# Sigmoids of the mixing stage made from tanh, gate columns moved forward in the input projection, forget-gate logarithm placed behind the decay chain

## The chip, the core and the metric

The kernel runs on one core of a Trainium2 chip. TensorE multiplies matrices into eight PSUM banks, VectorE (DVE) and ScalarE (ACT) do elementwise work, GpSimd (POOL) does elementwise work in SBUF and issues some DMAs, SyncE (SP) issues the weight loads. Each engine runs its own list of instructions; semaphores order them. The metric is the device time of one launch in microseconds.

## The reference

Two layers of a hybrid encoder over 288 tokens, 256 of a prompt and 32 of a second request. In each layer, with width 1024:

```python
x = x + 0.5 * swiglu(rmsnorm(x, n1), f1g, f1u, f1d)
z = rmsnorm(x, nm) @ w_in_l
logf = jax.nn.log_sigmoid((ff + b_f).astype(F32))
o_fox = (o_fox.reshape(B, T, FOX_WIDTH) * jax.nn.sigmoid(fg)).astype(x.dtype)
...
w = -jax.nn.softplus(-(w0 + jnp.tanh(wd) @ w_up).astype(F32)) - 0.5
decay = jnp.exp(-jnp.exp(w))
a = jax.nn.sigmoid((a0 + ad @ a_up).astype(F32))
g = (jax.nn.sigmoid(gd) @ g_up).astype(F32)
kk = kk * lax.rsqrt(jnp.maximum(jnp.sum(kk * kk, axis=-1, keepdims=True), 1e-24))
k = k * (1.0 + (a - 1.0) * k_a.astype(F32).reshape(RWKV_HEADS, HEAD_DIM))
bonus = jnp.sum(r * k * r_k.astype(F32)[None, None], axis=-1, keepdims=True) * v
...
o = head_norm(o, RET_GN_EPS).reshape(B, T, RET_WIDTH) * jax.nn.silu(g.astype(F32))
...
x = x + jnp.concatenate([o_fox, o_rwkv.astype(x.dtype), o_ret.astype(x.dtype)], axis=-1) @ w_out_l
x = x + 0.5 * swiglu(rmsnorm(x, n2), f2g, f2u, f2d)
```

The three mixers are a forgetting attention of 8 heads (fox), an RWKV-7 time mixing of 4 heads, and a chunkwise retention of 4 heads. A last gate and a norm end the layer.

## The kernel before

Everything is float32 and stands feature by feature in the partitions, with the 288 tokens along the free dimension. A weight matrix comes in slots of 1 MB through a ring of four buffers. Each product is made of three: a slot is cast to a high part (ScalarE) and a remainder (VectorE, in the projection GpSimd), and so is the activation, and TensorE adds high by high, high by low and low by high.

The input projection has 31 blocks of 128 columns (`NZ`). For block n, `z_cast(n)` on ScalarE (L563) makes the high part of the weights, `rest(n)` on GpSimd (L419) the remainder, TensorE does 24 matmuls (`z_slot`, L1320 and L1323) into one of four banks, and `z_copy(n)` on ScalarE (L575) brings the bank into the tile `zT`. There are two pairs of weight buffers, so the cast of block n waits until TensorE is through block n-2, and GpSimd waits for the cast. On ScalarE the first 16 blocks are a loop of two turns (L577). The last four blocks, 27 to 30, are the output gate of the attention (`Z_FG`); ScalarE takes Exp of their negative instead of a copy (L574).

Work of the RWKV mixer is put by hand between the blocks:

- VectorE shifts blocks 0 to 6 in time (L871 to L879). ScalarE then takes Exp of the small block (L593, `esm`), VectorE makes a sigmoid of it (`sigmoid_of`, L851 and L852) and scales it (L885, `lowin`). TensorE's low-rank products for decay and learning rate wait for it behind block 17 (L1337).
- VectorE prepares the keys (L890) and the forget gate (L894 to L896). ScalarE squares the keys (L596), then takes Exp and Ln for the forget gate (L599, L600), and casts block 19.
- ScalarE takes Exp of the four low-rank outputs (L605, `e_low`, tile `sig4`). TensorE goes on with blocks 18 and 19, makes the gate's low-rank products and the head sums of the squared keys (L1348), and goes on with blocks 20 to 23.
- VectorE: the forget-gate chain (L898 to L910: logarithm, three cumulative sums, a copy, two products into `foxL`), which the attention wants much later; then the sigmoids of `sig4` (L851, L852), the logarithm of the decay and its cumulative sums (L917 to L924), the clamp of the key norm (L930, which signals `kln`), and, once ScalarE has the inverse norm (L617, L618), the keys (L932 to L936) and the input of the bonus (L939, which signals `bonin`).
- TensorE, behind block 23: two rotation products for the retention (L1355), which wait for `kln` since they take the clamped banks, then two bonus products (L1364), which wait for `bonin`; then blocks 24 to 29, two more rotations and block 30. ScalarE takes the four decay exponentials (L622 to L627) between its blocks 22 and 23.

After that come transposes, the products inside a chunk, four levels of a triangular inverse (TensorE L1429 to L1441, VectorE L1016 to L1027, where `sigmoid_of` is also applied to the four blocks of `Z_FG`, one in each level), the recurrence over nine chunks, the attention and the output projection. VectorE's `link` makes an instruction wait for the end of the one before it.

## Time and profile before

| | |
|---|---|
| median of three runs | 1635.5 us (1634.3 to 1638.49) |
| profiled execution, its own time | 1637.02 us |
| its span from first to last instruction | 1635.4 us |
| TensorE busy | 1539.1 us, 94% of the span |
| VectorE busy | 867.2 us, 53% |
| ScalarE busy | 593.8 us, 36% |
| GpSimd busy | 196.8 us, 12% |
| mean granted clock of TensorE | 0.920 |

A row of the trace in order of time has the start and the duration in microseconds, the engine, the line of the kernel, the operation, output and inputs with their shapes, how many instructions are merged in the row, and in brackets how long the engine was idle before and what ended that. Instructions of one line that follow each other stand in one row, with the time from the first's start to the last's end. A busy TensorE is not TensorE at its peak: its matmuls are pipelined and their ends are modelled. The granted clock is 1.0 at 2.4 GHz and 0.5 at 1.2 GHz.

### The profile page before, as it was taken

To read this page: it belongs to the slowest core of one execution; us is meant where nothing else is said; L and a number is where in the kernel's file an instruction comes from. 1 tells how busy PE (TensorE), PEld (TensorE's weight loads), DVE (VectorE), ACT (ScalarE), POOL (GpSimd) and SP (SyncE) were. 2 spreads that over 40 slices of the span, in tenths; PEclk is the share of its full clock that TensorE was granted. 3 is DMA by queue.
4 is the path that set the end of the run, shared out by engine and by line. 5 is a ranking of instruction groups with operands and counts; after the bars stand their busy time and mean duration, and the time that the engine had idled before them with its cause. 6 is when DMAs were issued, how large, how long until landed. Compare 5 with 4: busy or idle time off the path is not lost. (4 is left out here: it accounts for less than half of the span.)

```text
span 1635.4 us, 27385 instructions
## 1 busy us (share of the span) xinstructions
PE 1539.1 (94%) x11276; PEld 1428.3 (87%) x11276; DVE 867.2 (53%) x1240; ACT 593.8 (36%) x871; POOL 196.8 (12%) x129
## 2 busy tenths in 40 slices
PE   7999999988989999999979999997899999999997
PEld 6999989877755899999979999897787568999997
DVE  4555344768444445553555553348773543555535
ACT  4334334441023444433443342445220334443324
POOL 1000017640020000000000000275400200000000
PEclk9999999988667999999989999999985779999999
DMA  7444433430010244444334444243300122444443
GB/s 300 157 162 172 154 129 129 155 114 20 11 59 27 101 156 173 161 158 177 133 134 154 166 168 156 102 157 126 133 1 11 59 75 107 145 164 156 178 158 133
DMA packets 32035, 209.81 MB, mean 128 GB/s; under 512 B 4392, under 2 KB 6072, under 8 KB 7752
## 3 DMA queue, kind: packets, MB, share of 16 engines
q1 hardware_dynamic: 29392, 200.39, 34.1%
q0 software_dynamic: 2560, 8.26, 1.4%
q8 instruction: 58, 0.95, 0.3%
q14 instruction: 25, 0.20, 0.0%
HBM read 204.54 MB, written 4.10 MB: 128 GB/s over the span
## 5 line engine op out<-in xcount | busy, mean ns | idle before, releaser
L792 DVE TENSOR_TENSOR split_w<-wc,split_w 128x2048 fp32r<-128x2048 f32 x140 | 320.6, 2292 | 374.4 <-ACT split_w L519 374.4
L519 ACT ACTIVATE split_w<-wc 128x2048 fp32r<-128x2048 f32 x140 | 268.4, 1917 | 540.5 <-PE bank L1252 341.7
L1246 PE MATMUL bank<-split_x,split_w 128*128 128x288 f32 x2816 | 399.1, 299 | 15.8 <-ACT split_x L525 15.8
L1246 PEld LDWEIGHTS bank<-split_x,split_w 128*128 128x128 f32 x2816 | 385.7, 190 | 21.0 <-ACT split_w L519 13.7
L1269 PE MATMUL bank<-split_x,split_w 128*128 (+1 forms) x2112 | 282.2, 295 | 0.0
L1269 PEld LDWEIGHTS bank<-split_x,split_w 128*128 128x128 f32 x2112 | 281.8, 188 | 0.0
L1252 PE MATMUL bank<-split_x,split_w 128*128 128x288 f32 x1408 | 202.2, 296 | 0.0
L1252 PEld LDWEIGHTS bank<-split_x,split_w 128*128 128x128 f32 x1408 | 192.6, 189 | 0.3 <-DVE split_w L792 0.3
L419 POOL TENSOR_TENSOR split_x<-wc,split_x 128x1024 fp32r<-128x1024 f32 x32 | 79.8, 2493 | 509.0 <-ACT split_x L563 509.0
L563 ACT ACTIVATE split_x<-wc 128x1024 fp32r<-128x1024 f32 x62 | 65.4, 1059 | 111.6 <-PE bank L1323 111.6
L1320 PE MATMUL bank<-split_h,split_x 128*128 128x288 f32 x496 | 84.4, 313 | 7.5 <-ACT split_h L568 7.4
L1320 PEld LDWEIGHTS bank<-split_h,split_x 128*128 128x128 f32 x496 | 74.0, 196 | 12.3 <-issue 9.0
L1320 PE MATMUL bank<-split_x 128*128 128x288 f32 x496 | 79.8, 305 | 0.0
L419 POOL TENSOR_TENSOR split_e<-wc,split_x 128x1024 fp32r<-128x1024 f32 x30 | 75.5, 2517 | 25.2 <-ACT split_x L563 25.2
L1320 PEld LDWEIGHTS bank<-split_x 128*128 128x128 f32 x496 | 72.8, 195 | 0.7
L818 DVE SCALAR_TENSOR_TENSOR et<-et,bank 128x288 f32<-128x288 f32 x88 | 40.0, 454 | 45.8 <-PE bank L1252 45.8
L1728 PE MATMUL bank<-split_x,split_w 128*128 128x288 f32 x384 | 53.0, 298 | 0.0
L1728 PEld LDWEIGHTS bank<-split_x,split_w 128*128 128x128 f32 x384 | 51.7, 189 | 1.1 <-ACT split_x L757 1.1
L411 POOL DMA_DIRECT2D extra<-srwkv_in x2 | 1.3, 658 | 359.0 <-issue 348.2
L1323 PE MATMUL bank<-split_h,split_x 128*128 128x288 f32 x256 | 40.4, 301 | 0.0
L1323 PEld LDWEIGHTS bank<-split_h,split_x 128*128 128x128 f32 x256 | 37.1, 195 | 0.0
L1323 PE MATMUL bank<-split_h,split_e 128*128 128x288 f32 x240 | 36.8, 296 | 0.0
(291 smaller groups left out, 1681.5 us busy)
## 6 DMA issues: line engine op xcount, KB each, us to landing
wc<-wcol SPq DMA_DIRECT2D x174, 1024.0 KB, 4.8
wc<-wfirst SPq DMA_DIRECT2D x12, 1024.0 KB, 4.9
con<-consts_in SPq DMA_DIRECT2D x1, 2230.0 KB
arena<-kc_in POOLq DMA_DIRECT2D x8, 256.0 KB, 3.1
arena<-vc_in POOLq DMA_DIRECT2D x2, 1024.0 KB, 5.1
xT<-x_in SPq DMA_DIRECT2D x2, 576.0 KB, 4.4
k_out<-zT POOLq DMA_DIRECT2D x8, 144.0 KB, 2.2
v_out<-zT POOLq DMA_DIRECT2D x8, 144.0 KB, 2.3
```

The costliest lines, as they stand in the source:

```text
L411: pool.dma_start(st[:, 0, :, :], srwkv_in[layer, 0]).then_inc(S["mixin"], 16)
L419: pool.tensor_tensor(lo, z_raw(n), hi, ALU.subtract).then_inc(S["zlo"], 1)
L519: act.activation(ws[s % 2][0], wc[:, p % RING, :], ACT.Copy).then_inc(S["cast"], 1)
L563: act.activation(zw[n % 2][0], z_raw(n), ACT.Copy).then_inc(S["zcast"], 1)
L792: dve.tensor_tensor(lo, wc[:, (POS_FFN[f] + s) % RING, :], hi, ALU.subtract).then_inc(S["wlo"], 1)
L818: dve.scalar_tensor_tensor(e, e, 0.5, bank[2 * (q % 4) + 1][:, 0:T], ALU.mult, ALU.mult)\
L1246: pe.matmul(o, hi[:, k, cs], x[:, k, :], start=(w == 0 and k == 0), stop=False)
L1252: mm = pe.matmul(o, lo[:, k, cs], h_hi[:, k, :], start=False, stop=(k == DB - 1))
L1269: return pe.matmul(bank[m][:, 0:T], w[:, kk, m * 128:m * 128 + 128], rhs, start=start, stop=stop)
L1320: pe.matmul(o, hi[:, k, :], x[:, k, :], start=(w == 0 and k == 0), stop=False)
L1323: mm = pe.matmul(o, lo[:, k, :], zh_hi[:, k, :], start=False, stop=(k == DB - 1))
L1728: mm = pe.matmul(bank[2 * s + cc][:, 0:T], w[:, k, cc * 128:cc * 128 + 128], x[:, k, :], start=(n == 0 and k == 0), stop=(n == 2 and k == ...
```

## The change

Sigmoids of the mixing stage are made as half of one plus tanh of half the argument. ScalarE's Exp of the negative becomes Tanh with a scale of 0.5; the addition of one and the reciprocal on VectorE (`sigmoid_of`) go. Where a multiplication follows, it becomes one instruction that adds one and multiplies; the factor 0.5 goes into a scaling that is there already. Since Tanh and Ln are in different activation tables, ScalarE loads a table ahead of the projection and another one behind the last of these Tanh.

The blocks of the projection are computed in another order (`Z_ORDER`): after blocks 0 to 6 the two retention gate blocks and the four attention gate blocks, then the rest of the retention, then the rest of the attention. ScalarE's loop over the first 16 blocks is written out. On VectorE the decay chain and the clamp stand ahead of the forget gate's logarithm and sums; on ScalarE the forget gate's Exp and Ln move behind the copies of the low-rank gate, between blocks 19 and 20; on GpSimd the wait for the logarithm and its DMA move from behind the remainder of block 21 to behind that of block 27.

```diff
+Z_ORDER = (*range(7), *range(Z_TG, Z_TG + 2), *range(Z_FG, Z_FG + 4), *range(Z_TQ, Z_TQ + 6), *range(Z_FQ, Z_FQ + 12))
@@ GpSimd
-                    for n in range(18, 22):
+                    for n in range(18, 28):
                         rest(n)
                     pool.wait_ge(S["lgf_ok"], 1)
                     pool.dma_start(logf_out[layer], lgf[0:8, :]).then_inc(S["zstore"], 16)
-                    for n in range(22, NZ):
+                    for n in range(28, NZ):
                         rest(n)
@@ ScalarE
-                    with act.Fori(0, 2) as i:
-                        for q in range(8):
-                            z_cast(q + 2, i)
-                            z_copy(i * 8 + q, q % Z_BANKS)
+                        z, o = Z_ORDER[n], bank[n % Z_BANKS][:, 0:T]
+                        if z >= Z_FG:
+                            act.activation(zT[:, z, :], o, ACT.Tanh, scale=0.5).then_inc(S["z_ev"], 1)
+                        else:
+                            act.activation(zT[:, z, :], o, ACT.Copy).then_inc(S["z_ev"], 1)
...
+                    act.preload_act_table_set("exp_and_others")
+                    for n in range(16):
+                        z_block(n)
                     act.wait_ge(S["small"], N_SHIFTED)
-                    act.activation(esm, zT[:, Z_SMALL, :], ACT.Exp, scale=col(C_SMALLSC)).then_inc(S["e_small"], 1)
+                    act.activation(esm, zT[:, Z_SMALL, :], ACT.Tanh, scale=col(C_SMALLSC)).then_inc(S["e_small"], 1)
                     z_block(16)
                     act.wait_ge(S["kraw"], 2)
                     act.activation(bhat, kkf, ACT.Square).then_inc(S["ksq"], 1)
-
-                    act.wait_ge(S["fu_ok"], 1)
-                    link(act.activation(fe[0:8, :], fe[0:8, :], ACT.Exp))
-                    act.activation(fe[0:8, :], fe[0:8, :], ACT.Ln, bias=col(C_ONE, slice(0, 8))).then_inc(S["fl_ok"], 1)
                     z_block(17)
-                    act.wait_ge(S["negp"], 1)
+                    act.wait_ge(S["halfp"], 1)
                     for i in range(4):
                         act.wait_ge(S["low_ps"], i + 1)
-                        act.activation(sig4[:, i, :], bank[4 + i][:, 0:T], ACT.Exp, scale=-1.0,
-                                       bias=negp[:, i:i + 1]).then_inc(S["e_low"], 1)
+                        act.activation(sig4[:, i, :], bank[4 + i][:, 0:T], ACT.Tanh, scale=0.5,
+                                       bias=halfp[:, i:i + 1]).then_inc(S["e_low"], 1)
+                    for b in range(2):
+                        act.activation(rgt[b], zT[:, Z_TG + b, :], ACT.Tanh, scale=0.5).then_inc(S["rgate"], 1)
+                    act.preload_act_table_set("natural_log_exp_and_others")
                     z_slot(9)
                     for b in range(2):
                         act.wait_ge(S["low_ps"], 5 + b)
                         act.activation(gate[:, b, :], bank[6 + b][:, 0:T], ACT.Copy).then_inc(S["gcp"], 1)
-                    for b in range(2):
-                        act.activation(rgt[b], zT[:, Z_TG + b, :], ACT.Exp, scale=-1.0).then_inc(S["rgate"], 1)
+                    act.wait_ge(S["fu_ok"], 1)
+                    link(act.activation(fe[0:8, :], fe[0:8, :], ACT.Exp))
+                    act.activation(fe[0:8, :], fe[0:8, :], ACT.Ln, bias=col(C_ONE, slice(0, 8))).then_inc(S["fl_ok"], 1)
                     z_slot(10)
@@ VectorE
-                    def sigmoid_of(e):
-
-                        link(dve.tensor_scalar(e, e, 1.0, None, ALU.add))
-                        link(dve.reciprocal(e, e))
...
                     dve.wait_ge(S["e_small"], 1)
-                    sigmoid_of(esm)
                     dve.tensor_scalar(dz[:, 0, :], esm, col(C_SMALLM), col(C_SMALLA), ALU.mult, ALU.add)\
                        .then_inc(S["lowin"], 1)
...
                     dve.tensor_tensor(fe[e8, :], fe[e8, :], fu[e8, :], ALU.min).then_inc(S["fu_ok"], 1)
+                    dve.wait_ge(S["e_low"], 4)
+                    lw, aa = sig4[:, 0:2, :], sig4[:, 2:4, :]
+                    link(dve.tensor_scalar(lw, lw, 0.5 * LOG_DECAY, 0.5 * LOG_DECAY, ALU.mult, ALU.add))
...
+                    link(dve.tensor_scalar(aa, aa, 0.5, 0.5, ALU.mult, ALU.add))
+
                     dve.wait_ge(S["fl_ok"], 1)
                     dve.scalar_tensor_tensor(lgf[e8, :], fu[e8, :], 0.0, fe[e8, :], ALU.min, ALU.subtract)\
                        .then_inc(S["lgf_ok"], 1)
...
-                    dve.wait_ge(S["e_low"], 4)
-                    sigmoid_of(sig4)
-                    lw, aa = sig4[:, 0:2, :], sig4[:, 2:4, :]
-                    link(dve.tensor_scalar(lw, lw, LOG_DECAY, None, ALU.mult))
-                    for b in range(2):
-                        dve.tensor_tensor_scan(lc[:, b, :], c("restart")[:, 0:T], lw[:, b, :], 0.0,
-                                               ALU.mult, ALU.add).then_inc(S["lcs"], 1)
...
-                        dve.tensor_scalar(khat[:, b, :], bank[4 + b][:, 0:T], 1e-24, None, ALU.max).then_inc(S["kln"], 1)
                     dve.wait_ge(S["rn"], 2)
                     link(dve.tensor_tensor(kkf, kkf, khat, ALU.mult))
...
                         dve.wait_ge(S["rgate"], b + 1)
-                        sigmoid_of(rgt[b])
-                        link(dve.tensor_tensor(zT[:, Z_TG + b, :], zT[:, Z_TG + b, :], rgt[b], ALU.mult))
+                        link(dve.scalar_tensor_tensor(zT[:, Z_TG + b, :], rgt[b], 1.0, zT[:, Z_TG + b, :],
+                                                      ALU.add, ALU.mult))
...
-                        sigmoid_of(fg[:, s - 1, :])
...
-                        dve.tensor_tensor(hT[rows, b, 0:TP], bank[4 + b % 2][rows, 0:TP], fg[rows, b, 0:TP], ALU.mult)\
+                        dve.scalar_tensor_tensor(hT[rows, b, 0:TP], fg[rows, b, 0:TP], 1.0, bank[4 + b % 2][rows, 0:TP],
+                                                 ALU.add, ALU.mult)\
                            .then_inc(S["fo_ok"], 1)
...
-                        link(dve.tensor_scalar(pq[:, e, 0:128], pq[:, e, 0:128], fm[:, 16 + 2 * e:17 + 2 * e], None, ALU.mult))
+                        link(dve.tensor_scalar(pq[:, e, 0:128], pq[:, e, 0:128], fm[:, 16 + 2 * e:17 + 2 * e], 0.5, ALU.mult, ALU.mult))
```

The retention's output product, the sample's attention and the second scaling get the same treatment, and the constants of the small block and the order of the weight columns on the host follow.

## Rows read from the trace of the kernel before

**Rows 1.** Waits of TensorE, 236 to 370 us: total, times, longest, in us.
```profile
PE bank L1364 <- DVE arena L939: 5.4, 2, 4.3
PE bank L1355 <- DVE arena L930: 4.3, 1, 4.3
PE bank L1337 <- DVE arena L885: 0.7, 1, 0.7
```
**Rows 2.** Stretches: length, busy time of PE, PEld, DVE, ACT, POOL, granted clock, DMA.
```profile
246.50:301.00 54.50, 54.50 (x409) 54.34 (x407) 23.08 (x15) 23.51 (x35) 41.56 (x17) 1.00 0.41 143
...
324.50:342.50 18.00, 8.31 (x25) 6.08 (x25) 15.94 (x21) 6.62 (x12) 4.96 (x2) 0.62 0.25 97
...
1134.50:1152.50 18.00, 8.45 (x29) 6.13 (x29) 15.94 (x21) 6.62 (x12) 4.96 (x2) 0.62 0.27 97
```
**Rows 3.** TensorE in order of time, first layer, blocks 20 to 24.
```profile
310.51 1.24 PE L1348 MATMUL bank<-arena,con 128*128 128x288 f32 x4
...
323.30 1.23 PE L1323 MATMUL bank<-split_h,split_e 128*128 128x288 f32 x8
328.78 2.29 PE L1355 MATMUL bank<-zT,con 128*128 128x288 f32 x4 [4.25 <-DVE arena L930]
335.38 1.30 PE L1364 MATMUL bank<-arena,con 128*128 128x288 f32 x2 [4.31 <-DVE arena L939]
337.80 1.33 PE L1364 MATMUL bank<-arena,con 128*128 128x288 f32 x2 [1.13 <-DVE arena L939]
338.51 2.54 PE L1320 MATMUL bank<-split_h,split_x 128*128 128x288 f32 x8
...
342.56 1.21 PE L1323 MATMUL bank<-split_h,split_x 128*128 128x288 f32 x8
```
**Rows 4.** VectorE in order of time, from the small block to the decay sums.
```profile
296.60 1.82 DVE L851 TENSOR_SCALAR arena<-arena 128x288 f32<-128x288 f32 x1 [10.37 <-ACT arena L593]
...
305.00 0.68 DVE L904 TENSOR_TENSOR_SCAN extra<-foxR,extra 8x256 f32<-8x256 f32 x1
305.71 3.24 DVE L905 TENSOR_TENSOR_SCAN extra<-foxR,extra 8x512 f32<-8x512 f32 x1
...
313.92 2.61 DVE L910 TENSOR_TENSOR foxL<-extra,con 8x2048 f32<-8x2048 f32 x2
...
317.25 7.35 DVE L852 RECIPROCAL arena<-arena 128x1152 f32<-128x1152 f32 x1
324.63 0.46 DVE L917 TENSOR_SCALAR arena<-arena 128x576 f32<-128x576 f32 x1
```
**Rows 5.** VectorE in order of time, from the clamp to the bonus input.
```profile
330.34 0.76 DVE L932 TENSOR_TENSOR arena<-arena 128x576 f32<-128x576 f32 x1 [1.61 <-ACT arena L618]
331.14 2.75 DVE L935 TENSOR_SCALAR arena<-arena,par 128x288 f32<-128x288 f32 x2
333.92 0.76 DVE L936 SCALAR_TENSOR_TENSOR zT<-arena,zT 128x576 f32<-128x576 f32 x1
334.71 3.04 DVE L939 SCALAR_TENSOR_TENSOR arena<-zT,par 128x288 f32<-128x288 f32 x2
```
**Rows 6.** GpSimd in order of time, two of its subtractions.
```profile
308.18 2.93 POOL L419 TENSOR_TENSOR split_x<-wc,split_x 128x1024 fp32r<-128x1024 f32 x1 [0.30 <-ACT split_x L563]
...
319.44 2.40 POOL L419 TENSOR_TENSOR split_e<-wc,split_x 128x1024 fp32r<-128x1024 f32 x1
```
**Rows 7.** ScalarE in order of time: a cast, the low-rank outputs, a table load.
```profile
246.58 1.06 ACT L563 ACTIVATE split_x<-wc 128x1024 fp32r<-128x1024 f32 x1 [5.09 <-PE bank L1323]
...
305.52 1.63 ACT L605 ACTIVATE arena<-bank,negp 128x288 f32<-128x288 f32 x4
...
576.59 1.28 ACT L528 ACT_TABLE_LOAD   x1
```
**Rows 8.** VectorE and TensorE in order of time, level stage.
```profile
392.80 1.95 DVE L852 RECIPROCAL zT<-zT 128x288 f32<-128x288 f32 x1
...
398.72 2.42 PE L1429 MATMUL bank<-arena 128*128 128x128 f32 x24
```

More of the change, by code:

```diff
@@ L124, in program @@
         par = sb("par", P, N_PARAM)
-        negp = sb("negp", P, 4)
+        halfp = sb("halfp", P, 4)
         nf = sb("nf", P, DB)
@@ L568, in _, with z_copy @@
                         act.activation(zh_hi[:, b, :], h1[:, b, :], ACT.Copy).then_inc(S["zh_hi"], 1)
-                    def z_copy(n, q):
+                    def z_copy(n):
                         act.wait_ge(S["z_ps"], n + 1)
-                        if isinstance(n, int) and n >= Z_FG:
-                            return act.activation(zT[:, n, :], bank[q][:, 0:T], ACT.Exp, scale=-1.0).then_inc(S["z_ev"], 1)
-                        return act.activation(zT[:, n, :] if isinstance(n, int) else zT[:, bass.ds(n, 1), :],
-                                              bank[q][:, 0:T], ACT.Copy).then_inc(S["z_ev"], 1)
-                    with act.Fori(0, 2) as i:
-                        for q in range(8):
-                            z_cast(q + 2, i)
-                            z_copy(i * 8 + q, q % Z_BANKS)
+                        z, o = Z_ORDER[n], bank[n % Z_BANKS][:, 0:T]
[3 more added lines that the diff above has]
+                            act.activation(zT[:, z, :], o, ACT.Copy).then_inc(S["z_ev"], 1)
                     def z_block(n):
@@ L584, in z_block @@
                             z_cast(n + 2)
-                        z_copy(n, n % Z_BANKS)
+                        z_copy(n)
                     def z_slot(s):
@@ L896, in _ @@
                     dve.tensor_tensor(fe[e8, :], fe[e8, :], fu[e8, :], ALU.min).then_inc(S["fu_ok"], 1)
+                    dve.wait_ge(S["e_low"], 4)
+                    lw, aa = sig4[:, 0:2, :], sig4[:, 2:4, :]
+                    link(dve.tensor_scalar(lw, lw, 0.5 * LOG_DECAY, 0.5 * LOG_DECAY, ALU.mult, ALU.add))
+                    for b in range(2):
+                        dve.tensor_tensor_scan(lc[:, b, :], c("restart")[:, 0:T], lw[:, b, :], 0.0,
+                                               ALU.mult, ALU.add).then_inc(S["lcs"], 1)
+                    dve.wait_ge(S["lcs"], 2)
+                    dve.tensor_tensor(eexc, lc, lw, ALU.subtract).then_inc(S["dexc"], 1)
+                    chunks = lc.rearrange("p b (n u) -> p (b n) u", u=CH)
+                    dve.tensor_tensor(eend.rearrange("p b (n u) -> p (b n) u", u=CH),
+                                      chunks[:, :, CH - 1:CH].to_broadcast([P, 2 * NCH, CH]), chunks,
+                                      ALU.subtract).then_inc(S["dend"], 1)
+                    for b in range(2):
+                        dve.wait_ge(S["kk_ps"], b + 1)
+                        dve.tensor_scalar(khat[:, b, :], bank[4 + b][:, 0:T], 1e-24, None, ALU.max).then_inc(S["kln"], 1)
+                    link(dve.tensor_scalar(aa, aa, 0.5, 0.5, ALU.mult, ALU.add))
                     dve.wait_ge(S["fl_ok"], 1)
@@ L1171, in _ @@
                         link(dve.reciprocal(fm[:, 30:31], fm[:, 29:30]))
-                        dve.tensor_scalar(ps_s[:, g, :], ps_s[:, g, :], fm[:, 30:31], None, ALU.mult).then_inc(S["spn"], 1)
+                        dve.tensor_scalar(ps_s[:, g, :], ps_s[:, g, :], fm[:, 30:31], 0.5, ALU.mult, ALU.mult)\
+                           .then_inc(S["spn"], 1)
                     for e in range(2):
@@ L1175, in _ @@
                         rows = slice(64 * e, 64 * e + 64)
-                        dve.tensor_tensor(hT[rows, 0:4, TP:T], bank[6 + e][rows, 0:128].rearrange("p (b t) -> p b t", b=4),
-                                          fg[rows, :, TP:T], ALU.mult).then_inc(S["so_ok"], 1)
+                        dve.scalar_tensor_tensor(hT[rows, 0:4, TP:T], fg[rows, :, TP:T], 1.0,
+                                                 bank[6 + e][rows, 0:128].rearrange("p (b t) -> p b t", b=4),
+                                                 ALU.add, ALU.mult).then_inc(S["so_ok"], 1)
                     out_lo(slice(0, 4), slice(TP, T), 2)
@@ L1814, in constants @@
     cols[:, C_KKB] = 15.0 * np.log(2.0)
-    cols[32:64, C_SMALLSC], cols[96:128, C_SMALLSC] = -2.0, -1.0
-    cols[32:64, C_SMALLM], cols[96:128, C_SMALLM] = 2.0, 1.0
-    cols[32:64, C_SMALLA] = -1.0
+    cols[32:64, C_SMALLSC], cols[96:128, C_SMALLSC] = 1.0, 0.5
+    cols[32:64, C_SMALLM], cols[96:128, C_SMALLM] = 1.0, 0.5
+    cols[96:128, C_SMALLA] = 0.5
     put("cols", cols)
@@ L1847, in in_blocks @@
     fox, rw, ret = 0, 2056, 2920
+    place = {block: n for n, block in enumerate(Z_ORDER)}
     def put(block, at, n, off=0):
-        out[..., block * P + off:block * P + off + n] = w[..., at:at + n]
+        for i in range(0, n, P):
+            to, size = place[block + i // P] * P + off, min(P, n - i)
+            out[..., to:to + size] = w[..., at + i:at + i + size]
     put(Z_SMALL, fox + 1536, 8)
@@ L1858, in in_blocks @@
     put(Z_V, rw + 544, 256)
-    put(Z_TQ, ret, 1024)
+    put(Z_TQ, ret, 768)
+    put(Z_TG, ret + 768, 256)
     put(Z_FQ, fox, 1536)
```

17 lines of the change are left out of this document (5 added, 12 removed).

## The prediction

> **What bounds the kernel now.** TensorE works nearly all the time, so I read first its list of waits over the first layer's projection and what follows [rows 1]. The reader is to see three waits on VectorE: 5.4 us in two pieces for the bonus product (L939), 4.3 us for the clamped key norm (L930), and 0.7 us for the low-rank input (L885). Then I read the busy time by stretch [rows 2]. In 246.5 to 301 us TensorE runs 409 matmuls in 54.5 us, 133 ns each; a block of the projection is 24 of them, 3.2 us. In 324.5 to 342.5 us it is busy for 8.31 of 18 us, with a mean granted clock of 0.62. The second layer shows the same stretch at the same distance (8.45 us, 0.62), so whatever is found counts twice. TensorE in order of time [rows 3] places this: block 23 (the 24th) ends at 324.5; the rotation products start at 328.78, the two bonus products at 335.38 and 337.80, and block 24 only at 338.51. The clock has fallen meanwhile: the first eight matmuls of block 24 take 2.54 us where eight take 1.2 elsewhere, and the block takes 4.05 us up to its last third at 342.56 where two thirds take 2.13.
>
> VectorE's timeline [rows 4] says why: the forget-gate chain holds it from 305.00 to 316.53, then the decay sigmoid (add and a reciprocal over 1152 columns, 7.35 us) until 324.63, and only then the decay sums and the clamp. What comes after the clamp up to the bonus products is [rows 5].
>
> **Low-rank input.** The reciprocal behind L851 goes. The remaining multiply-add takes the place of L851, which started at 296.60 and, beside GpSimd, ended at 298.4 [rows 4]. TensorE is busy without a break up to 301.0 [rows 2] and then waits 0.7 us for this input [rows 1], so only those 0.7 us are gained.
>
> **Decay chain ahead of the forget gate.** On ScalarE the four activations of the low-rank outputs took 1.63 us from 305.52 [rows 7], behind the forget gate's Exp and Ln. These two now come later; with the cast for block 19 first (from 301.2) the four start near 302.5 and end near 304.1. VectorE then has one 576-column multiply-add (0.46 us, L917), two scans, two subtractions (together 2.8 us, from 325.13 to 327.9 as L917's row and the clamp show) and the clamp. A pass of GpSimd stands in the way once, up to 304.7, so the sums are ready near 308. The clamp needs TensorE's head sums, which stand behind block 19: L1348 started at 310.51 [rows 3], now about 309.9, done near 310.7. The clamp is ready at about 311.5 instead of 328.7, and TensorE needs it only at the end of block 23, now about 323.8. The first wait, 4.3 us, goes, and the rotation products run at the full clock (1.1 us, not 2.3), until 324.9.
>
> **What is late next.** Between the clamp and the bonus product VectorE now has the forget-gate chain, which before stood ahead of both. It is 11.5 us as it ran (305.00 to 316.53 [rows 4]). L905, a scan over 512 columns, took 3.24 us where 256 columns took 0.68, so at most 1.4 are work and 1.9 are waiting. Between its end (308.95) and L910's start (313.92) stand only a scan of 32 columns and a copy of 800; by L904 and L917 (576 columns in 0.46) their work is some 0.9 us, so 4 more were lost. They ran beside GpSimd's subtractions (2.4 us each, one per block [rows 6]); the reverse shows too: the subtraction at 308.18 took 2.93. Without these losses the chain is about 5.7 us. Behind it stand L932, L935 (two), L936 and L939's first: 0.76 + 0.75 + 0.76 + 0.5 = 2.8 us of work, while [rows 5] has 2.75 for L935 and 3.04 for L939 where these met GpSimd.
>
> In which case is the moved chain? TensorE now does not stop between 311 and 324, so GpSimd subtracts for 2.4 of every 3.2 us. I walked the chain through the passes for blocks 21 to 25 (they follow the end of blocks 19 to 23 by 1.1 us of cast, for 25 also by the four decay exponentials, which ScalarE does first): 0.5 us of multiply-add ends near 313.0 after pass 21; the log, scan 1 and scan 2 fit before and over the start of pass 22, to 315.5; scan 3 and the copy follow it, to 318.4; the long product (2.3 us) lies ahead of or behind pass 23, the last product and L932 around pass 24, to about 326; L935 waits for pass 25, which ends near 328.3; then 0.4 + 0.8 + 0.5 us. The inverse norm that L932 waited for (1.6 us [rows 5]) is no part of it now: ScalarE makes it after block 21, by about 320.6. The bonus input is there at about 330.2; putting one instruction on the other side of a pass gives 329.4 to 331.2. No pass 26 can follow, since its cast needs block 24. The first bonus product thus starts at 330.2 instead of 335.38, 5.2 us earlier. The second input follows 0.4 us behind with no GpSimd pass between, so the wait of 1.1 us at 337.80 goes as well: 6.3 us in a layer. TensorE idles for 5.3 us, not much more than the 4.25 after which the clock was low before, so I leave block 24's loss at the low clock (4.05 less 2.13, 1.9 us) as it was; between none and twice that are the bounds.
>
> The Trainium skill, SBUF — State Buffer, section "Who interferes with whom", says that VectorE instructions with two SBUF inputs or in a two-port mode and GpSimd's exclude each other for a whole instruction. L905's row agrees. By that rule the moved chain cannot run at its free speed, and the sum is the 6.3 us above; without it, it would be the first rival below. The rule speaks against the place that the change gives to the forget chain.
>
> **Edits that I cost at nothing.** Two table loads per layer, 1.28 us each [rows 7]: the first falls in ScalarE's wait of 5.09 us before 246.58, the second follows the four activations and two more for the retention gates (0.4 each) and ends near 306.2, before a cast of 1.06 us that TensorE wants only at 310.7; without this cover they would be 5.1 us in both layers. The four reciprocals of the output gate in the level stage (1.95 us each [rows 8]): TensorE's products there follow each other without a gap (L1429 at 398.72 shows no wait), so they were hidden, and nothing returns; likewise the two retention gates, done before the second rotation wants VectorE. The combined instructions that replace a multiplication, and the factor 0.5 that rides on a scaling: L936, a combined form, takes the 0.76 us of the plain L932 [rows 5], and L935 has two operations already. ScalarE's loop of 16 blocks is written out: each block leaves it waiting. The log's DMA on GpSimd's queue moves behind the subtraction of block 27; behind it wait only passes 28 to 30, each ready 1.06 + 2.4 us after the block two before it, and wanted 3.2 + 2.1 us after that; 1.8 us are to spare, so from 0 to 1 us. The gate columns are ahead, and what is last in the projection is all waited for as a whole, as before.
>
> **Sum.** The profiled execution took 1637.0 us (span 1635.4). Two layers at 6.3 us are 12.6: 1624.4. The median of the runs shown is 1.5 us below that execution, so 1623 us. Downstream of block 24 TensorE has work up to the transposes and everything shifts along; but the clock falls and rises again in the later stages of mixing, and the moments may shift. The two layers' stretches differ little in [rows 2]; I allow 2 us per layer either way. With the 329.4 to 331.2 above that makes 1617 to 1629 the forecast's own range.
>
> **Rivals.**
> *The chain runs free.* If GpSimd gives way each time, or its passes lie otherwise, the bonus input is ready before the rotation ends, TensorE does not stop, and the clock stays up: block 24 starts at about 326.1 instead of 338.51, and 1.9 us are not lost at the low clock: 14.3 us in a layer, 1607 us. For it: the chain has 5.7 + 2.8 us of work and 12 us of time; against it [rows 4 to 6].
> *The wait only moves.* If the chain loses still more (a pass at each of its nine linked instructions), the bonus products start where they did, and only 0.7 + 1.1 us of a layer are won: 1632 us. Against it: no pass after 25 can come.
> *Slower: the clock stays low.* There is now one pause of 5 us. If the 1.2 GHz level lasted to the end of block 30, seven blocks would take 6.4 us instead of 3.2, 22.4 us in a layer less the 1.9 already there; against the 6.3 won that is 14 slower, 1664 us. It decides as soon as more than two further blocks stay low. For it: the mean clock of 0.62 in both layers. Against it: in [rows 3] the clock was back 4 us after the work began (eight matmuls in 1.21 us at 342.56), although two pauses went ahead.
> That the change does nothing at all would need an unseen wait on the same products; its reciprocals stand plainly on the path, so I give it no more than a part of the second rival.
>
> **Chances.** Forecast 0.74, free chain 0.12, wait only moves 0.09, slower by the clock 0.05. A measurement of this kernel tells about 0.3% (5 us) from no change. Of the forecast nearly all (0.73) lies past that bound, with the free chain 0.85 faster; same 0.10; slower 0.05. For the range I reach from 1610 (some of the losses of the chain not there) to 1631 (most of the gain eaten by wait or clock): outside are the far end of the free chain and the slower case.
>
> **What the profile will show.** Right: no wait of TensorE at the rotation, one wait at the first bonus product of 4 to 6.5 us, block 24 about 6 us earlier relative to the projection's start; VectorE's copy and scans of the forget chain beside GpSimd passes at 2 to 3 us each. Wrong: a wait at the rotation still, a wait at the bonus over 8 or under 2 us, a wait of TensorE on GpSimd's subtraction, or on ScalarE's cast behind the table load.

## The result and the profile after

The changed kernel takes 1621.1 us (median; 1620.9 to 1622.4) where the kernel before, run beside it, takes 1636.3 (1634.3 to 1638.5): a ratio of 0.9909, 95% interval 0.9892 to 0.9926, so 15 us less. The forecast was 1623, in a range of 1610 to 1631, and its sum was 12.6 us. The profiled execution has a span of 1619.5 us (before: 1635.4).

TensorE's waits in the first layer's projection and what follows (the stretch of [rows 1]; total, times, longest, in us):

```profile
PE bank L1363 <- DVE arena L935: 4.9, 1, 4.9
...
PE bank L1322 <- POOL split_e L420: 0.2, 1, 0.2
```

and in the second layer:

```profile
PE bank L1363 <- DVE arena L935: 3.7, 1, 3.7
PE bank L1322 <- POOL split_e L420: 1.4, 1, 1.4
```

Of the waits in [rows 1] those at the clamp (4.3 us) and at the low-rank input (0.7 us) are gone, and the bonus product has one wait instead of two. A small wait on GpSimd is new. Left out are a wait of 3.7 us at the stage's first block and one of 0.9 us at the first products inside a chunk, which the kernel before has too. Without these two, TensorE waited 10.4 us in the first layer's stage and now waits 5.0.

The busy time by stretch, with the columns of [rows 2]:

```profile
246.50:299.00 52.50, 52.50 (x401) 52.50 (x400) 22.80 (x17) 23.33 (x36) 41.58 (x17) 1.00 0.41 145
321.50:339.50 18.00, 13.14 (x72) 12.04 (x72) 17.52 (x22) 4.64 (x8) 8.05 (x3) 0.81 0.33 117
1124.70:1142.70 18.00, 14.32 (x80) 13.22 (x81) 17.21 (x19) 4.14 (x7) 8.67 (x4) 0.81 0.33 117
```

The 18 us around the rotation and the bonus hold 13 to 14 us of TensorE's work where they held 8.3 to 8.5, and the mean granted clock is 0.81 instead of 0.62. TensorE in order of time, from the last third of block 23 to the first blocks behind the bonus (compare [rows 3]):

```profile
321.33 1.32 PE L1322 MATMUL bank<-split_h,split_e 128*128 128x288 f32 x8 [0.16 <-POOL split_e L420]
322.49 1.13 PE L1354 MATMUL bank<-zT,con 128*128 128x288 f32 x4
328.48 2.26 PE L1363 MATMUL bank<-arena,con 128*128 128x288 f32 x4 [4.86 <-DVE arena L935]
330.12 2.54 PE L1319 MATMUL bank<-split_h,split_x 128*128 128x288 f32 x8
332.45 2.01 PE L1319 MATMUL bank<-split_x 128*128 128x288 f32 x8
334.31 1.22 PE L1322 MATMUL bank<-split_h,split_x 128*128 128x288 f32 x8
```

The rotation follows block 23 without a gap and takes 1.13 us (before: 2.29 at the lower clock). Behind the one pause of 4.86 us block 24 runs at the low level first, as before: 4.19 us up to its last third, 4.05 before.

VectorE from the low-rank input to the bonus input (compare [rows 4, 5]):

```profile
294.95 1.81 DVE L880 TENSOR_SCALAR arena<-arena,con 128x288 f32<-128x288 f32 x1 [10.10 <-ACT arena L594]
...
302.41 0.90 DVE L894 TENSOR_SCALAR arena<-arena 128x576 f32<-128x576 f32 x1 [1.92 <-ACT arena L602]
...
309.00 0.94 DVE L907 TENSOR_SCALAR arena<-bank 128x288 f32<-128x288 f32 x2 [2.79 <-PE bank L1347]
...
312.43 1.21 DVE L918 TENSOR_TENSOR_SCAN extra<-foxR,extra 8x512 f32<-8x512 f32 x1
...
313.99 2.71 DVE L921 COPY foxR<-extra 8x800 f32<-8x800 f32 x1
316.73 4.82 DVE L923 TENSOR_TENSOR foxL<-extra,con 8x2048 f32<-8x2048 f32 x2
321.48 0.74 DVE L928 TENSOR_TENSOR arena<-arena 128x576 f32<-128x576 f32 x1
322.25 4.73 DVE L931 TENSOR_SCALAR arena<-arena,par 128x288 f32<-128x288 f32 x2
327.02 0.76 DVE L932 SCALAR_TENSOR_TENSOR zT<-arena,zT 128x576 f32<-128x576 f32 x1
327.81 0.95 DVE L935 SCALAR_TENSOR_TENSOR arena<-zT,par 128x288 f32<-128x288 f32 x2
```

and GpSimd's subtractions over the same time (each is called a pass):

```profile
313.87 2.38 POOL L420 TENSOR_TENSOR split_x<-wc,split_x 128x1024 fp32r<-128x1024 f32 x1 [3.10 <-ACT split_x L564]
317.07 4.20 POOL L420 TENSOR_TENSOR split_e<-wc,split_x 128x1024 fp32r<-128x1024 f32 x1 [0.81 <-ACT split_x L564]
321.24 3.21 POOL L420 TENSOR_TENSOR split_x<-wc,split_x 128x1024 fp32r<-128x1024 f32 x1
324.41 2.41 POOL L420 TENSOR_TENSOR split_e<-wc,split_x 128x1024 fp32r<-128x1024 f32 x1
```

The clamp (L907) is done at 309.9 us, 12.5 us ahead of the rotation that wants it. From then on the forget chain and the bonus input's steps run against GpSimd. The copy (L921) and the first of the long products (L923) show both sides: the copy ends at 316.7, just behind GpSimd's pass, which ends at 316.3; the product takes over at once, the next pass, begun at 317.07, stretches to 4.20 us, and the short second product ends only when that pass has. The two instructions of L931 then end with the passes that end at 324.45 and 326.82.

The gain by stage, from the start of the projection's first block to the first transpose behind the last (TensorE in order of time): 125.1 us to 117.7 in the first layer, 123.9 to 118.9 in the second, so 7.5 and 5.0. Of the 15.6 us by which TensorE's last instruction ends earlier in the two profiles, 12.5 are thus in the two stages that the change touches, 0.8 ahead of the first, and 2.4 in the parts behind the stages. That the layers differ is not the work of the change: from the first block to the start of block 17's last third, where TensorE waits for nothing in either kernel, the two layers took 61.2 and 60.4 us before and take 60.3 and 61.6 now. From there to the first transpose they took 63.9 and 63.5 us and take 57.4 and 57.3: 6.5 and 6.2 us less.

### The profile page after: what moved, and what is told of

The parts are those of the page before. It is cut to its first block and busy times, and to the rows that moved or that the text cites. A ratio compares the mean times of both kernels' runs of the same rounds, so it can differ in the third digit from the quotient of the medians.

```text
span 1619.5 us, 27305 instructions
## 1 busy us (share of the span) xinstructions
PE 1534.6 (95%) x11276; PEld 1428.5 (88%) x11276; DVE 820.8 (51%) x1210; ACT 597.8 (37%) x875; POOL 201.2 (12%) x129
## 5 line engine op out<-in xcount | busy, mean ns | idle before, releaser
L420 POOL TENSOR_TENSOR split_e<-wc,split_x 128x1024 fp32r<-128x1024 f32 x30 | 80.1, 2670 | 17.4 <-ACT split_x L564 17.4
```

Of the source, the lines that this page charges most:

```text
L420: pool.tensor_tensor(lo, z_raw(n), hi, ALU.subtract).then_inc(S["zlo"], 1)
```

## The experiments

The theory at this point: VectorE's work up to the bonus product, stretched by GpSimd's subtractions, is what TensorE waits for, and the tanh form won because VectorE has a 7.35-us reciprocal less there. Rivals: the new order alone brought the gain; or the forget chain only stands in a bad place, and another place frees the 5 us that are left; or the parts behind the stages gained of themselves.

**The order alone.** The kernel before, with the forget chain behind the decay chain and ScalarE's Exp and Ln behind the low-rank outputs, as in the change, and the reciprocals kept.

```diff
@@ VectorE
-                    dve.wait_ge(S["fl_ok"], 1)
-                    dve.scalar_tensor_tensor(lgf[e8, :], fu[e8, :], 0.0, fe[e8, :], ALU.min, ALU.subtract)\
...
                     dve.wait_ge(S["e_low"], 4)
                     sigmoid_of(sig4)
...
+                    dve.wait_ge(S["fl_ok"], 1)
+                    dve.scalar_tensor_tensor(lgf[e8, :], fu[e8, :], 0.0, fe[e8, :], ALU.min, ALU.subtract)\
...
                     dve.wait_ge(S["rn"], 2)
                     link(dve.tensor_tensor(kkf, kkf, khat, ALU.mult))
```

> The kernel before with the new order alone: decay chain and clamp ahead of the forget-gate chain on VectorE, the forget gate's Exp and Ln and the logarithm's DMA where the change puts them; all sigmoids still with their reciprocals, columns as before. If the reciprocal over 1152 columns (7.35 us) matters as much as the order: the clamp at about 320 us, in time for the rotation, the forget chain from there to 330, the bonus input at 333 to 334 instead of 335.2; 2 to 3 us in a layer, 1629 to 1632. If the order alone pays: 1621 to 1624. If it pays nothing alone: 1634 to 1637.

Measured: 1635.8 us, ratio 0.9993 (0.9982 to 1.0004): nothing that the time shows. TensorE's waits, first layer:

```profile
PE bank L1364 <- DVE arena L939: 9.9, 1, 9.9
...
PE bank L1337 <- DVE arena L885: 0.6, 1, 0.6
```

The wait at the rotation is gone, and the one at the bonus is 9.9 us: what the first lost, the second gained (5.4 + 4.3 before). VectorE's and GpSimd's orders of time show the same work in another order:

```profile
308.12 7.35 DVE L852 RECIPROCAL arena<-arena 128x1152 f32<-128x1152 f32 x1
...
324.51 3.38 DVE L922 TENSOR_TENSOR_SCAN extra<-foxR,extra 8x512 f32<-8x512 f32 x1
327.93 2.45 DVE L923 TENSOR_TENSOR_SCAN extra<-foxR,extra 8x32 f32<-8x32 f32 x1
```

```profile
308.70 2.39 POOL L419 TENSOR_TENSOR split_x<-wc,split_x 128x1024 fp32r<-128x1024 f32 x1 [1.23 <-ACT split_x L563]
311.89 2.39 POOL L419 TENSOR_TENSOR split_e<-wc,split_x 128x1024 fp32r<-128x1024 f32 x1 [0.81 <-ACT split_x L563]
```

**The tanh form with the forget chain first.** The changed kernel, with VectorE's forget chain ahead of the decay chain again. ScalarE's Exp and Ln, which that chain needs, stay late, where the change puts them.

```diff
@@ VectorE
+                    dve.wait_ge(S["fl_ok"], 1)
+                    dve.scalar_tensor_tensor(lgf[e8, :], fu[e8, :], 0.0, fe[e8, :], ALU.min, ALU.subtract)\
...
                     dve.wait_ge(S["e_low"], 4)
                     lw, aa = sig4[:, 0:2, :], sig4[:, 2:4, :]
...
-                    dve.wait_ge(S["fl_ok"], 1)
-                    dve.scalar_tensor_tensor(lgf[e8, :], fu[e8, :], 0.0, fe[e8, :], ALU.min, ALU.subtract)\
...
```

> The changed kernel with VectorE's forget-gate chain back ahead of the decay chain (ScalarE's order and the tanh stay). If the order on VectorE is what pays, the clamp comes at about 327 us of the first layer instead of 310: a wait of 4 to 5 us at the first rotation and again 3 to 5 at the bonus, 5 to 6 us of the gain of a layer lost, 1631 to 1637. If the sigmoids made without a reciprocal are what pays, whatever the order, 8 us of VectorE are gone here too and the time stays within 4 us of the changed kernel, 1619 to 1625.

Measured: 1630.0 us, ratio 0.9959 (0.9945 to 0.9973). TensorE's waits, the same in both layers:

```profile
PE bank L1363 <- DVE arena L935: 6.6, 2, 5.4
...
PE bank L1354 <- DVE arena L924: 2.8, 1, 2.8
```

So some 6 of the 15 us are left when VectorE's order is undone. The two stages are 2.6 and 1.2 us shorter than before here, 1.8 and 0.6 in the run with the order alone. This is not the tanh form by itself, though: the chain stands first on VectorE and waits for ScalarE, which makes Exp and Ln as late as in the change.

```profile
311.76 0.95 DVE L893 SCALAR_TENSOR_TENSOR extra<-et 8x288 f32<-8x288 f32 x1 [9.44 <-ACT et L613]
```

VectorE stands idle for 9.44 us there; the same instruction waited 1.08 us before, and started at 304.41. The tanh form with both engines in their old order was not run. An estimate from [rows 4]: without the 8.1 us between the end of L910 (316.53) and L917 (324.63), the clamp, ready at 328.7 before, would be ready near 320.6, ahead of the 324.5 at which TensorE wants it. The estimate leaves out the further table loads of that order and the passes that VectorE would then meet. So the order is shown to bring nothing alone; whether the tanh form needs it stays open.

**The forget chain behind the bonus input.** The changed kernel, with VectorE's chain moved behind L935, and the same with ScalarE's inverse key norm two blocks earlier.

```diff
@@ VectorE
-                    dve.wait_ge(S["fl_ok"], 1)
-                    dve.scalar_tensor_tensor(lgf[e8, :], fu[e8, :], 0.0, fe[e8, :], ALU.min, ALU.subtract)\
...
                         dve.scalar_tensor_tensor(bon[:, b, :], r[:, b, :], pa("rk", b), k[:, b, :],
                                                  ALU.mult, ALU.mult).then_inc(S["bonin"], 1)
 
+                    dve.wait_ge(S["fl_ok"], 1)
+                    dve.scalar_tensor_tensor(lgf[e8, :], fu[e8, :], 0.0, fe[e8, :], ALU.min, ALU.subtract)\
...
                     dve.wait_ge(S["exps"], 4)
```

> The changed kernel with VectorE's whole forget-gate chain (logarithm, sums, copy, two products into foxL) moved once more, behind the two bonus inputs. If that chain is what the bonus products still wait for (4.9 and 3.7 us in the two layers of the changed kernel), the wait there falls to 2 us or less, the 1.4 and 0.2 us that TensorE waits for GpSimd's remainder of block 23 go too, and the clock need not fall behind block 23: up to 7 us in a layer, 1607 us. But VectorE and GpSimd shut each other out, and the chain now stands ahead of the seven products that the second rotation waits for: I count some 336 us for its end and 8 us of work behind it against a need at about 344, so a new wait of up to 5 us there; with that 1612 to 1618. Rival (the wait only moves): the whole 5 us come back at the second rotation, 1621. Rival (something else holds the bonus): the wait at the bonus products stays over 3.5 us and the time is within 2 us of the changed kernel.

ScalarE's edit in the second kernel:

```diff
+                    for b in range(2):
+                        act.wait_ge(S["kln"], b + 1)
...
                     z_slot(10)
-                    for b in range(2):
-                        act.wait_ge(S["kln"], b + 1)
...
                     z_block(22)
```

> As the kernel with the forget-gate chain behind the bonus inputs, and ScalarE makes the inverse key norm ahead of its block 20 instead of behind its block 21, so about 7 us earlier. If VectorE's order is all that the bonus waits for, the bonus input is ready before the first rotation ends, no wait and no fall of the clock there; the forget chain fills the time up to the decay exponentials (near 322 us) and ends near 329, the products for the second rotation near 340 before their need at 344: 1607 to 1612. Rival (the wait only moves): a wait of 4 us or more at the second rotation, 1615 to 1621.

Measured: 1626.3 us, ratio 0.9933 (0.9908 to 0.9958), and 1625.1 us, 0.9926 (0.9909 to 0.9942): neither is better than the change, and both lie above what was expected (1612 to 1618 and 1607 to 1612). Waits of TensorE, first the chain moved, then with the early norm, in both layers alike:

```profile
PE bank L1363 <- DVE arena L918: 2.9, 2, 1.7
PE bank L1354 <- DVE et L961: 2.4, 1, 2.4
```

```profile
PE bank L1354 <- DVE et L961: 5.0, 1, 5.0
```

With the early norm the bonus wait is gone and 5.0 us stand at the second pair of rotations instead. VectorE is late there because the chain and then the products for the chunks met GpSimd's passes:

```profile
328.33 4.82 DVE L934 TENSOR_TENSOR foxL<-extra,con 8x2048 f32<-8x2048 f32 x2
...
336.73 2.88 DVE L941 TENSOR_TENSOR arena<-zT,arena 128x576 f32<-128x576 f32 x1
339.64 2.99 DVE L942 SCALAR_TENSOR_TENSOR arena<-arena 128x576 f32<-128x576 f32 x1
```

TensorE's waits in a stage are 5.0 and 5.1 us in the change, 5.3 and 5.0 in these two: moving the whole chain inside the stage moves the wait and doesn't shorten it. That the second of them is 4 us slower than the change is not in its stages, which are as long (235.9 us together, 236.5 in the change), but behind them; the last experiment comes back to it.

**A part of the chain out of the stage.** If that holds, work has to leave the stage. The chain's two products (8x2048 and 8x256) are wanted much later, so they go behind the level stage, where VectorE waited 4.46 us for TensorE. They read the copy of the sums.

```diff
@@ VectorE
-                    for q0, k0, n in ((0, 0, TP), (TP, TP + PAST, TS)):
-                        dve.tensor_tensor(foxL[e8, :, q0:q0 + n],
-                                          cbuf[e8, k0:k0 + n].unsqueeze(1).to_broadcast([8, FOX_H, n]),
...
+                    w = con[32:40, CONSTS["fox8"][0]:CONSTS["fox8"][0] + 8]
+                    for q0, k0, n in ((0, 0, TP), (TP, TP + PAST, TS)):
+                        dve.tensor_tensor(foxL[e8, :, q0:q0 + n],
+                                          foxR[32:40, k0:k0 + n].unsqueeze(1).to_broadcast([8, FOX_H, n]),
...
                     dve.wait_ge(S["uac"], 6)
```

> The changed kernel with one more part moved: the forget gate's last two products (8x2048 and 8x256, which held VectorE from 316.7 to 321.5 beside GpSimd) wait until the level stage is done, where VectorE was idle for 4.5 us; they read the copy of the sums instead of the sums. Theory (the forget chain beside GpSimd's subtractions is what the first bonus product waits for): the bonus input comes near 324.5, TensorE's wait of 4.9 and 3.7 us falls to under 1.5 us in both layers, block 24 follows at full clock or nearly, and each projection stage is 4 to 6 us shorter than in the changed kernel: 1608 to 1613 us. Rival (the wait only moves, as it did with the whole chain behind the bonus input): TensorE waits about 5 us in the second rotation or at the transposes instead, 1620 to 1622 us.

Measured: 1616.8 us, ratio 0.9877 (0.9857 to 0.9897): 4.3 us under the change, where 8 to 13 were expected. TensorE waits 2.9 us at the bonus, in two pieces, in both layers. VectorE's order of time says why:

```profile
322.17 0.96 DVE L922 TENSOR_TENSOR arena<-arena 128x576 f32<-128x576 f32 x1 [2.44 <-ACT arena L619]
323.17 2.80 DVE L925 TENSOR_SCALAR arena<-arena,par 128x288 f32<-128x288 f32 x2
326.00 0.76 DVE L926 SCALAR_TENSOR_TENSOR zT<-arena,zT 128x576 f32<-128x576 f32 x1
326.79 3.04 DVE L929 SCALAR_TENSOR_TENSOR arena<-zT,par 128x288 f32<-128x288 f32 x2
```

With the chain shorter, ScalarE's inverse norm is late by 2.44 us, and two of the steps behind it meet a pass each. So the norm went two blocks ahead here too, with the same edit on ScalarE as above:

> As the run with the late products, and ScalarE makes the inverse key norm two blocks earlier, so that VectorE does not wait for it behind the shorter chain. Theory: no wait at the bonus product, none in the rotations, the clock stays at 2.4 GHz through the stage, 1605 to 1612 us, 0 to 2 us a layer under the run before. Rival: the norm is not what VectorE waits for, and the time is that of the run before within 1 us; or the two casts that the norm now stands ahead of come late, and TensorE waits 1 to 2 us for a remainder in blocks 20 to 22.

Measured: 1610.8 us, ratio 0.9842 (0.9823 to 0.9860). The stages take 111.7 and 115.2 us. In the first TensorE waits 0.8 us for the bonus input and block 24 runs at full clock; in the second one more step meets a pass, and TensorE in order of time shows what that costs:

```profile
1121.79 0.72 PE L1363 MATMUL bank<-arena,con 128*128 128x288 f32 x2 [0.93 <-DVE arena L929]
1124.21 0.75 PE L1363 MATMUL bank<-arena,con 128*128 128x288 f32 x2 [1.70 <-DVE arena L929]
1124.59 2.06 PE L1319 MATMUL bank<-split_h,split_x 128*128 128x288 f32 x8
```

1.8 us more of waiting, and nearly 2 us more in the bonus products and block 24 at the low level, make the 3.5 us between the layers. The moved products take 2.62 us behind the level stage, inside VectorE's old wait, and the chunks' first instruction follows the level stage as closely as before.

**The rest of the chain behind the bonus input**, on top of the last kernel: log, three scans and copy, some 3.2 us of work.

```diff
@@ VectorE
-                    dve.wait_ge(S["fl_ok"], 1)
-                    dve.scalar_tensor_tensor(lgf[e8, :], fu[e8, :], 0.0, fe[e8, :], ALU.min, ALU.subtract)\
...
                     dve.wait_ge(S["rn"], 2)
...
+                    dve.wait_ge(S["fl_ok"], 1)
+                    dve.scalar_tensor_tensor(lgf[e8, :], fu[e8, :], 0.0, fe[e8, :], ALU.min, ALU.subtract)\
...
                     dve.wait_ge(S["exps"], 4)
```

> As the run with the late products and the early norm, and what is left of the forget chain on VectorE (the log, three scans and the copy, 3.2 us of work) also stands behind the bonus input. Theory (TensorE waits at the bonus product only because this chain is ahead of it, and there are now some 4 us to spare before the second rotation): no wait at the bonus product, none in the rotations, the clock at 2.4 GHz from block 24 on, both projection stages near 111 us, as the first layer of the run before nearly had: 1603 to 1610 us. Rival (the wait moves again): VectorE comes late at the second rotation or at the transposes by 1 to 3 us in both layers, 1609 to 1613 us.

Measured: 1609.6 us, ratio 0.9840 (0.9823 to 0.9858), the fastest here, 1.6% under the kernel before and 0.7% under the change. TensorE no longer waits at the bonus; 1.7 us are left at the second pair of rotations:

```profile
PE bank L1354 <- DVE et L955: 1.7, 1, 1.7
```

The stretches of 18 us from the rotation on are full, at the full clock, in both layers:

```profile
323.50:341.50 18.00, 18.00 (x131) 17.58 (x130) 17.66 (x13) 7.41 (x12) 13.45 (x7) 1.00 0.44 161
1118.90:1136.90 18.00, 18.00 (x131) 17.58 (x130) 17.66 (x13) 7.41 (x12) 13.46 (x7) 1.00 0.42 158
```

Both stages take 112.2 to 112.3 us, against 117.4 to 119.0 in the change. Theory and rival each had a part: no wait at the bonus, and 1.7 us of it moved. By the median it is level with the kernel before it; their intervals overlap.

**The reciprocals of the level stage.** The changed kernel, with four additions and four reciprocals over 288 columns back on VectorE between the levels of each layer, written to scratch.

```diff
                                 dve.tensor_tensor(four(tt, j), four(tt, j), d_t, ALU.add).then_inc(S["lvl"], 1)
+                        link(dve.tensor_scalar(et[:, 0, :], fg[:, s - 1, :], 2.0, None, ALU.add))
+                        link(dve.reciprocal(et[:, 0, :], et[:, 0, :]))
```

> The changed kernel with four additions and four reciprocals over 288 columns put back into VectorE's level stage of each layer, where the sigmoid of the output gate was (the results go to scratch and are not used). Theory (they were hidden, so taking them out brought nothing): 1620 to 1623 us, the level stage's span as in the changed kernel within 0.3 us. Rival (they stood on the path to the level products): each of the four costs up to its 1.95 us in both layers, up to 16 us, 1625 to 1637 us.

Measured: 1620.8 us, ratio 0.9900 (0.9879 to 0.9922), the time of the change. They are there (VectorE's groups in the level stage):

```profile
L1024 DVE RECIPROCAL et<-et 128x288 f32<-128x288 f32 x3 | 5.9, 1953 | 0.1
```

(three of the four lie in the window), and the levels take TensorE 26.1 us from first to last, 26.2 without them. They were hidden.

**The change once more, unchanged.**

> The changed kernel once more, unchanged, beside the other three. Theory (the gain of 15 us is 12.5 us in the two projection stages, 0.8 us ahead of them, and some 2 us that depend on where the low-clock stretches of the later stages fall): ratio 0.990 to 0.992; the two stages again 7.5 and 5.0 us shorter than before within 0.5 us, while the parts behind them may differ by 1 to 2 us. Rival (the 2 us behind the stages belong to the change too): the stages from the transposes to the end are again shorter by 2 to 2.5 us in all, in the same places.

Measured: 1621.6 us, ratio 0.9907 (0.9887 to 0.9926). TensorE's waits in the first layer:

```profile
PE bank L1363 <- DVE arena L935: 3.9, 1, 3.9
...
PE bank L1322 <- POOL split_e L420: 1.4, 1, 1.4
```

This is the pattern that the second layer had; here the second layer has the other (4.8 and 0.4 us). The stages are 6.2 and 6.4 us shorter than before, 12.6 together. The way from the first stage's end to the second's start is 3.0 us shorter, the way behind the second 1.9 us longer, where the first profile had 2.4 shorter and 0.1 longer. The first block started 0.6 us later than before here, and 0.8 us earlier in the first profile. So what lies outside the stages moves by 2 to 3 us from one execution to the next. The run with the whole chain behind the bonus input and the early norm shows how far one stretch goes, the same 104 matmuls of the attention in layer 1 and in layer 2:

```profile
468.58:497.39 28.81, 26.53 (x104) 15.05 (x104) 17.00 (x55) 11.23 (x37) 0.00 (x0) 0.86 0.00 1
1265.72:1302.45 36.73, 34.67 (x104) 18.93 (x105) 17.38 (x55) 11.02 (x37) 0.00 (x0) 0.64 0.00 1
```

The granted clock was 0.86 in the one and 0.64 in the other; in the change both layers take 31.2 us for it. The part behind the second stage, in which the second row stands, is 4.9 us longer in that profile than in the change; its stages are not.

That the medians differ by 15 us and the stages by 12.5 leaves 2 to 3 us. The eleven profiles together say a little about them. The way between the stages takes 685.7 us before and 685.1 with the chain behind the bonus input, but 682.4 to 683.5 in the other nine, among them the order alone, with its reciprocals in place (682.4). Behind the second stage eight take 448.7 to 449.2 us, the kernel before among them; the order alone (451.1), the change again (450.9) and the run with the two rows above (453.9) take longer. So in these profiles the 2.4 us do not go with the tanh form. Whether the change gained them steadily or the profiled executions happened to fall so stays open.

Stage lengths and TensorE's waits in them, from the first block to the first transpose, without the 3.7 us at the first block (the kernel before, run beside each, had medians of 1636.3 to 1636.9):

| kernel | layer 1, us (waits) | layer 2, us (waits) | median, us |
|---|---|---|---|
| before | 125.1 (10.4) | 123.9 (10.2) | 1636.3 |
| order alone | 123.4 (10.5) | 123.2 (10.5) | 1635.8 |
| tanh, forget chain first | 122.6 (9.3) | 122.7 (9.3) | 1630.0 |
| chain behind bonus | 119.3 (5.3) | 119.7 (5.3) | 1626.3 |
| ... and early norm | 118.4 (5.0) | 117.5 (5.0) | 1625.1 |
| the change | 117.7 (5.0) | 118.9 (5.1) | 1621.1 |
| the change again | 119.0 (5.3) | 117.4 (5.2) | 1621.6 |
| late products | 115.7 (2.9) | 115.7 (2.9) | 1616.8 |
| ... and early norm | 111.7 (0.8) | 115.2 (2.6) | 1610.8 |
| ... and the rest behind bonus | 112.3 (1.7) | 112.2 (1.7) | 1609.6 |

## Why the prediction was right, and where it was not

**The low-rank input**: 0.7 us a layer expected; the wait [rows 1] is gone in both layers. L880 started at 294.95 and ended at 296.8, long before 299.3, where TensorE wants it.

**The decay chain ahead.** Sums ready near 308 and the clamp at 311.5 were expected; they were ready at 306.2 and 309.9. The rotation doesn't wait and runs at the full clock, as written. Two table loads stayed hidden: no wait on a cast behind one appears.

**What is late next.** This carried the sum, and the walk through GpSimd's passes held nearly step by step: log, scans 1 and 2 done at 313.6 (315.5 expected), copy at 316.7 (318.4), L928 at 322.2 (L932 of before, 326), both instructions of L931 behind a pass each up to the one for block 25, which ended at 326.8 (328.3). All of it lies 1.5 to 2 us early, or 4 at L928, mostly since TensorE itself was 1.3 us early at the rotation. That was luck of this execution: 0.8 us of it is the earlier start of the stage, which the repetition doesn't show, and most of the rest are the faster blocks of the last section. The bonus product started at 328.5 for 330.2, 0.9 us under the lower end of its range (329.4). TensorE's wait was 4.9 us for 5.3 expected, and the second wait of 1.1 us went, as the step said. Block 24's loss at the low level stayed: 1.9 us expected, 2.1 found (4.19 less 2.13). Two signs came in part: the bonus wait is 3.7 us in the second layer, under the 4 that were named; and of the copy and the three scans only the copy in the first layer (2.71 us) and the short scan in the second (2.50) met a pass, the others ran as fast as alone. In the repetition the stages gave 6.2 and 6.4 us for the 6.3 of the sum.

**What was missing**: a wait of TensorE on GpSimd, which the prediction named as a sign of being wrong. The walk let VectorE wait for GpSimd and forgot the reverse in its sum, although [rows 6] has it (2.93 us for 2.40): the long product held up the pass for block 23's remainder, which took 4.20 us (5.42 in the second layer), and TensorE stood 0.2 and 1.4 us for it. The sum of the waits stayed the same, since the bonus wait was the shorter for it (4.9 + 0.2, 3.7 + 1.4). The Trainium skill's page SBUF — State Buffer, section "Who interferes with whom", has the rule for both sides: whoever issues first keeps the shared port pair for the whole instruction. The rows of L923 and of the pass at 317.07 agree.

**The sum.** 12.6 us expected and 12.5 (then 12.6) found in the stages; behind block 17 it is 6.5 and 6.2 us for the 6.3 of each layer, so the fit is one of the mechanism and not of the sum alone. The median went down by 15; the 2 to 3 us of difference are the open point of the last experiment, within the 2 us per layer that the prediction allowed.

**The rivals.** The free chain (1607 us) did not come: VectorE and GpSimd did exclude each other. The runs with late products show that the figure was near the right price for a TensorE that doesn't stop there: 1609.6 us, with 1.7 us of waiting left in each layer. *The wait only moves* was wrong for the change, since 10.4 us of waiting became 5.1, but right for the order taken alone, and for the moves of the whole chain inside the stage. The low clock in block 24 lasted no longer than before.

**The edits costed at nothing**: the level stage's reciprocals are shown to be worth nothing; the rest (combined instructions, the loop written out, the order of the columns, the log's DMA) left no wait of its own in the trace, and was not run apart.

## What to carry to other kernels

An order can be worth nothing by itself and still go well with a shortening, since it only moves the wait (here from the rotation to the bonus product): try them together before the order is dropped. To price the shortening by itself, put the order back on every engine: with VectorE's alone put back, VectorE waited 9.4 us for ScalarE, and the run priced that too. When a helper engine and the one that is late hold each other up, count all instructions of both up to the last thing that TensorE wants, not only the chain in front of the next wait; if the total is too long, moving work inside the stage only moves the wait, and work that is wanted later has to leave it. What a pause costs is the pause and the low clock behind it: the same stage took 111.7 us and 115.2 with 1.8 us of waiting between them.

## What the hardware showed beside that

- Not every instruction of VectorE is held up by GpSimd. In the run with the order alone the reciprocal takes its 7.35 us with two whole passes of 2.39 us inside it, neither longer than when alone, and the clamps, which read a bank, take 0.44 us each in the middle of a pass. The copy of 8x800 has one input as well, and took 0.57 us alone and 2.71 beside a pass; scans and two-input products wait too. So the tanh form takes out the one long instruction that was immune, and leaves those that are not.
- The price of being held up hardly depends on the instruction here: a scan of 32 columns, 0.27 us alone, took 2.45, about the length of the pass that it met.
- Some nine blocks of the projection ran at 3.12 us each instead of 3.20, in the first layer in one profile of the change (401 matmuls in 52.50 us, 131 ns each, for 133 in [rows 2]) and in the second layer in the repetition, at a granted clock of 1.00 in both. That is 0.6 to 0.8 us of a stage; what makes it is not known, and in the other layer of either profile little more than a block ran so.
